# Constant matrix products added ahead of jobs in the mixers of a hybrid decoder step

## What is computed

```python
def mixer(h, lp, st):
    proj = h @ lp['w_in']
    ...
        S_h, o_h = chunk_scan(hgrn_chunk, jnp.zeros((B, H_HGRN, HGRN_DK, HGRN_DV), F32), args_h)
    ...
        (C_m, n_m, m_m), o_m = chunk_scan(mlstm_chunk, init, (q_m, k_m, v_m, ig, lf))
    ...
            o, lse = swa_prompt(q_s[:, :, hs], k_s[:, :, hs], v_s[:, :, hs], win, dil)
    ...
    mix = jnp.concatenate([out_h, out_m, out_s], axis=-1).astype(h.dtype)
    return mix, new_st
```

## Time and profile before

| | us |
|---|---|
| median of 3 runs | 2786.8 (2784.9 to 2788.0) |
| the profiled execution | 2787.2 |
| its span, first to last instruction | 2785.4 |
| mean granted clock | 0.802 |
| first mixers, scores to samples, from the span's start | about 196 to 582 |
| second mixers | about 1257 to 1650 |

### The profile page before, as it was taken

How to read it: one execution, slowest core, us unless ns; L and a number is a source line. 1 busy time by engine, 2 the same in 40 slices (tenths; PEclk the granted TensorE clock), 3 DMA queues, 4 the chain that set the end, 5 groups by cost and what they waited for, 6 DMA issues and landing times.

```text
span 2785.4 us, 38888 instructions
## 1 busy us (share of the span) xinstructions
PE 2360.4 (85%) x15227; PEld 2098.1 (75%) x15227; DVE 1104.0 (40%) x1731; ACT 842.2 (30%) x1211; POOL 620.5 (22%) x323
## 2 busy tenths in 40 slices
PE   6997468776999995998439767899999999999996
PEld 5985266576999994996237556789888898988984
DVE  1113583521110111112576442366474654747542
ACT  3113223223222212112233212435243352533521
POOL 3420340023443442430160011012121121211210
PEclk9995555578999997996555558789898898988986
DMA  3240100011232243221000001145363553635520
GB/s 140 91 137 1 38 1 1 1 64 51 93 98 79 94 148 121 91 90 69 25 14 1 1 34 62 52 153 172 101 204 108 161 162 105 210 104 160 164 90 32
DMA packets 60928, 245.03 MB, mean 88 GB/s; under 512 B 9116, under 2 KB 9852, under 8 KB 60028
## 3 DMA queue, kind: packets, MB, share of 16 engines
q1 hardware_dynamic: 54496, 227.28, 24.8%
q10 hardware_dynamic: 6332, 16.34, 1.6%
HBM read 234.62 MB, written 19.41 MB: 91 GB/s over the span
## 4 chain that ended last, share of the span: by engine, by line
issue 38%; PE 34%; POOL 12%; DVE 10%; ACT 3%; DMA 2%; ACTq 1%; POOLq 0%; DVEq 0%; SPq 0%
PE psum L916 14%; PE psum L956 13%; POOL wlo L486 5%; POOL xlo L361 5%; PE psum L961 2%; PE psum L937 2%; PE psum L1367 2%; DMA wraw<-in_w_in 1%; POOL xnl L492 1%; DVE r_att L1706 1%; PE psum L1420 1%; PE psum L1342 1%; DMA cst<-in_cst 0%; PE psum L1422 0%; DVE r_w L1673 0%
## 5 line engine op out<-in xcount | busy, mean ns | idle before, releaser
L486 POOL TENSOR_TENSOR wlo<-wraw,whi 128x1024 fp32r<-128x1024 f32 (+1 forms) x122 | 304.9, 2501 | 584.4 <-ACT whi L585 584.4
L916 PE MATMUL psum<-xnh,whi 128*128 128x260 f32 x1824 | 373.1, 286 | 56.3 <-POOL wlo L486 21.3
L1420 PE MATMUL psum<-xg,xhi 128*128 128x320 f32 x1408 | 385.8, 316 | 19.7 <-POOL xlo L361 14.3
L361 DVE TENSOR_TENSOR xlo<-xraw,xhi 128x1024 fp32r<-128x1024 f32 (+2 forms) x224 | 282.4, 1264 | 249.4 <-ACT xhi L874 247.5
L1422 PE MATMUL psum<-xg,xlo 128*128 128x256 f32 x1408 | 377.9, 282 | 0.0
L916 PE MATMUL psum<-xnh,wlo 128*128 128x260 f32 x1824 | 370.9, 285 | 0.0
L916 PE MATMUL psum<-xnl,whi 128*128 128x260 f32 x1824 | 370.8, 285 | 0.0
L874 ACT CAST xhi<-xraw 128x1024 fp32r<-128x1024 f32 (+1 forms) x240 | 270.8, 1129 | 270.6 <-PE psum L1422 270.2
L361 POOL TENSOR_TENSOR xlo<-xraw,xhi 128x640 fp32r<-128x640 f32 (+2 forms) x80 | 167.8, 2098 | 815.9 <-ACT xhi L874 815.9
L916 PEld LDWEIGHTS psum<-xnh,whi 128*128 128x128 f32 x1824 | 285.1, 191 | 59.9 <-issue 31.0
L1420 PEld LDWEIGHTS psum<-xg,xhi 128*128 128x128 f32 x1408 | 266.2, 189 | 25.7 <-issue 19.6
(11 more groups left out here) (410 smaller groups left out, 3479.3 us busy)
## 6 DMA issues: line engine op xcount, KB each, us to landing
xraw<-in_moe_gu SPq DMA_DIRECT2D x176, 512.0 KB, 4.2
xraw<-in_moe_dn SPq DMA_DIRECT2D x64, 704.0 KB, 5.4
wraw<-in_w_in SPq DMA_DIRECT2D x54, 512.0 KB, 3.4
wraw<-in_ffn_gu SPq DMA_DIRECT2D x44, 512.0 KB, 3.5
wraw<-in_ffn_dn SPq DMA_DIRECT2D x16, 704.0 KB, 4.1
wraw<-in_w_out SPq DMA_DIRECT2D x16, 512.0 KB, 3.5
out_cache_s<-in_cache SPq DMA_DIRECT2D x4, 2040.0 KB
a_ck<-in_ck ACTq DMA_DIRECT2D x2, 3072.0 KB, 11.7
```

The costliest lines, as they stand in the source:

```text
L361: eng.tensor_tensor(xlo[n % RWX][:, c0:c1], xraw[n % RWX][:, c0:c1], xhi[n % HIX][:, c0:c1].bitcast(F32), ALU.subtract).then_inc(made_, 1)
L486: pool.tensor_tensor(wlo[u % SPL][:, 0:cols], wraw[u % RAW][:, 0:cols], whi[u % SPL][:, 0:cols].bitcast(F32), ALU.subtract).then_inc(lo_ma ...
L916: ins = pe.matmul(out[:, s, :], w[:, k * cols:(k + 1) * cols], x[:, k, s * H2:(s + 1) * H2], start=(k == 0 and first), stop=(k == kt - 1 a ...
L1420: pe.matmul(epart(n), xhi[n % HIX][:, k * P:(k + 1) * P], x_[:, k, :], start=(k == 0), stop=False, skip_group_check=True)
```

## The change

A method `idle(n)` of `Job` multiplies the identity with `mkr` n times into the first 256 columns of the job's own bank. The job's products overwrite these columns afterwards. It is called ahead of the jobs `pv` (12), `kh` (12), the first `at` job of levels 0 to 6 (14), `md` (8) and `mo` (8), in both layers. In the levels the job of the first head is now made ahead of the wait for `lv_made`, with the constant products between its wait for the bank and that one. The wait for `mask_made`, which `mlstm` had, is also made at the start of `window`.

```diff
+                def idle(self, n):
+
+                    for _ in range(n):
+                        pe.matmul(self.out(0, 2 * P), mkr[:, 0, :], mkr[:].rearrange("p a c -> p (a c)"), start=True, stop=True,
+                                  skip_group_check=True)
...
             def window(li):
+                pe.wait_ge(S("mask_made"), 1)
...
                     j = Job(li, "pv", n)
+                    j.idle(12)
                     taken(pe, li, "pt", n, 1 if n < 2 else 0)
...
                     j = Job(li, "kh", c)
+                    j.idle(12)
...
                     if l < LVL:
+                        j = Job(li, "at", 0, l)
+                        j.idle(14)
                         pe.wait_ge(S("lv_made"), LVL * li + l + 1)
...
-                        j = Job(li, "at", h, l)
+                        if h or l == LVL:
+                            j = Job(li, "at", h, l)
...
                     j = Job(li, "md", h)
+                    j.idle(8)
...
                     j = Job(li, "mo", h)
+                    j.idle(8)
                     taken(pe, li, "mqk", h)
```

## The result

The changed kernel takes 2803.5 us (median of 15 runs, 2790.4 to 2817.2) against 2785.7 for the kernel before, measured beside it: ratio 1.0064, 95% interval 1.0049 to 1.0079, or some 18 us slower. The forecast was 55 us slower. The direction and the range held; the size was three times too large.

What follows compares the result with a forecast made beforehand. PE was taken to bound three mixer stages and to be level with DVE in HGRN's levels. Terms 3.5 + 2.5 + 7 + 14.5 = 27.5 us a layer, 55 in both: 2787 + 55 = 2842 us, range 2780 to 2890.

Steps and rivals of the forecast that it cites:

- The price of the products: All bursts: 0.213 us a product at 1.2 GHz, 0.118 at 2.4; 55 us a layer, after cover by waits, without a rise.
- The levels' term: HGRN's seven levels: bursts mostly at 1.2 GHz, part of the products behind them at 2.4; +7 us a layer.
- mLSTM's: mLSTM: two uncovered bursts of 8 a head, 1.2 GHz for nine tenths of the stage; +14.5 us a layer.
- the window's: Window stage, six bursts of 12: half taken between +13.7 (1.2 GHz) and -6.9 (2.4 GHz); +3.5 us a layer.
- the states': HGRN's states and the diagonal: first burst covered, clock rises behind the second; +2.5 us a layer.
- What raises the clock: All bursts: expected to raise the clock where 128-row work stands beside them, 64-row work to lose it; busy PE not enough.
- The fall at 1276: Layer 1's window: clock fell from 1.00 to 0.50 amid gap-free score products, taken as evidence against a lasting high clock.
- the signs that I named: Profile after: mLSTM head about 10.9 us at 0.50, clock changing in kh and window, levels 7 to 8 us apart.
- all at 2.4: Window stage's lower bound: with everything at 2.4 GHz, 6.9 us a layer shorter than before the change.
- No burst raises the clock: Rival for all bursts: they are paid at 1.2 GHz, 55 us a layer, 2897 us; chance 0.11, including a 2873 us variant.
- The clock stays up: Rival for both mixers: bursts keep the clock high, -19 us a layer, outputs up to -13 more; 2745 us, chance 0.14.
- A wash (2787): Rival for all bursts: they lie in PE's waits or the clock pays for them; 2787 us, chance 0.06.

Runs made afterwards that it cites:

- e5_rows5: The changed kernel with all its bursts, but constant products of 5 rows in place of 128; 2904.7 us, ratio 1.0438.
- e1_levels: The changed kernel with only the bursts of 14 ahead of HGRN's levels, the others left out; 2779.8 us, ratio 0.9972.
- e10_levels7: e1_levels with bursts of 7 products in place of 14; 2800.8 us, ratio 1.0060.
- e2_mlstm: The changed kernel with only mLSTM's bursts of 8 (ahead of md and mo), the others left out; 2807.0 us, ratio 1.0072.
- e3_window: The changed kernel with only the bursts of 12 ahead of the pv jobs, the others left out; 2786.3 us, ratio 1.0003.
- e4_states: The changed kernel with only the bursts of 12 ahead of the kh jobs, the others left out; 2784.6 us, ratio 1.0005.
- e7_outputs: e1_levels with a burst of 14 added ahead of each of HGRN's five output jobs; 2785.7 us, ratio 1.0009.
- e9_first24: e1_levels with 24 products ahead of level 0 in place of 14, the other levels unchanged; 2780.4 us, ratio 0.9992.
- e8_best: e1_levels with one burst of 15 added ahead of the first kh job; 2779.7 us, ratio 0.9986.
- e11_levels_again: The same kernel as e1_levels, measured once more in another sitting; 2783.2 us, ratio 0.9995.
- e6_mlstm12: e2_mlstm with bursts of 12 products in place of 8; ratio 1.0030, +9 us.
- e12_mlstm16: e2_mlstm with bursts of 16 products in place of 8; 2794.6 us, ratio 1.0037.

## Why the prediction was right and wrong

The price of the products was right, and so were direction and range. What failed is what the clock gives back, and with it all four terms of the sum: +27.5 us a layer, where the four parts alone measured +8.4. The levels' term is the largest miss (+7 against -2.9 and, measured again, -0.4); mLSTM's was +14.5 against 10.7, the window's +3.5 and the states' +2.5 against 0.3 each.

- **The price of a product: right.** 0.213 us a product at 1.2 GHz gave 55 us a layer for no rise; e5_rows5 took 58.6 in layer 0. A cold head of mLSTM was put at 10.9 us and took 11.0. The first burst of the states is covered, as forecast: the first `su` starts 4.8 us after the keys are there in after (359.06 to 363.86) and 4.7 in before.
- **What raises the clock: right in kind, no rule.** The forecast took rows 5 and 6 to say that operands of 128 rows raise it and a busy PE alone doesn't; e5_rows5 against after bears that out for these bursts. The Trainium skill ("TensorE: Matmul & The Clock Gate", section "Why this matters for your kernels") advises to keep TensorE busy without gaps. By that rule e5_rows5 would have run at full rate; its trace disagrees, with 58.50 of 58.50 us busy at 0.50. The fall at 1276 was misread: in the earlier trace rows it stands between 14 products with vt and the transposes, 1.6 us behind the last scores, and not in their midst. So it doesn't show that 64-row work loses the clock.
- **The levels' term (+7 a layer): wrong in sign.** Two steps failed. "Each burst follows 64-row work and is itself likely still at 1.2" doesn't hold for 14 products a level: the clock stays up through the 64-row products for five levels (after, layer 0, from 402.9 on), and a level with its burst takes 4.9 us, near the 4.5 that the forecast had as its best. And the time behind the last factors was put at nothing: in e1_levels DVE sets the pace up to there, as forecast, but behind them 1.9 us a layer are to be had. Of the signs that I named, levels "about 7 to 8 us apart" throughout appear in e10_levels7 alone.
- **mLSTM (+14.5): right in mechanism, a term mis-sized.** I took 2.4 GHz for a tenth of the stage. In e2_mlstm the mean clock from the first gate products to the samples is 0.61, in after 0.62 and 0.55 over the stage, so between a tenth and a quarter. With e2_mlstm's share of 0.22 the forecast's own bounds (+17.0 to -10.3) give 11.0, an estimate beside the 10.7 measured.
- **Window (+3.5) and states (+2.5): mis-sized.** Alone 0.3 a layer each, which is within what these runs can't tell from nothing. In the window half of the way to "all at 2.4" was taken. In e3_window the mean clock is 0.85 and 0.83, two thirds of the way; from the forecast's bounds (+13.7 to -6.9) that gives -0.3, an estimate. In after it is 0.69 with the same bursts. Why the clock is up more in one execution than in another stays open. In e4_states' profile states and diagonal take 1.4 and 1.2 us more than in before, counted from the first burst: the diagonal gained 1.9 us where 1 was taken.
- **The rivals.** "No burst raises the clock" is e5_rows5, and no other kernel. "The clock stays up" fits most of the levels of e1_levels and layer 1's outputs in e7_outputs, in part of the executions. A wash (2787) is what window and states are by themselves.

The fastest kernels of the study have bursts ahead of the levels and none in mLSTM, window or outputs: medians 0.8 to 5.8 us under before (e1_levels in two sittings, e9_first24, and e8_best with its one burst more). All lie on the same side (ratios 0.9972 to 0.9995), but only e1_levels' first sitting lies past the 0.2% that the prediction took as the least to be told.

## What to carry to other kernels

A constant product put in to lift the clock has one price and two outcomes: compare the engine's time per round, burst included, at either clock with the pace that the next engine sets. In the levels that was 8.8 or 4.9 us against DVE's 6.3, in mLSTM 11.0 against PE's own 7.54, or 6.4 against 8.40, and the dose decided which: try a longer burst before giving up on one, and a shorter one is not the safe choice. Compare a round only with the same round of the kernel before, and look at several executions. Look also for the stretch in which the faster engine can show at all; here it was the two microseconds behind DVE's last factors.

## What the runs showed of the hardware

- A busy PE is not enough: bursts of 128 rows raised the clock, for part of the time, in all stages that the change put them in, bursts of five rows with the same count and columns left it at 0.50 (e5_rows5, mLSTM and levels). Nor are 128 rows enough: the gather, four of whose five products have them, stayed at 0.50 for 25.50 us.
- In these stages the length of a burst decided, not that bursts recur: with 7 a level the levels' products were at 1.2 GHz throughout, with 14 the mean clock of the stage was 0.70 to 0.88 (after, e1_levels, e8_best, e11_levels_again); e2_mlstm with 8 had four of five gate products at 1.2 GHz in each layer, e6_mlstm12 one and two, e12_mlstm16 one and none.
- Forty instructions of 64 rows and 64 columns take 5.62 us at 1.2 GHz and 3.1 at 2.4, so these small products follow the clock nearly in full (a factor of 1.8). The window's score products of 64 rows and 128 columns don't: a pair starts the next product after 0.76 us at either clock (before, layer 1, from 1270.27 and from 1278.25).
- The same instructions come out at different clocks from one execution, or one layer, to the next: the seven levels with 14 products took 38.4, 38.7, 41.8 and 44.5 us, the window stage with its bursts 48.6 and 55.9.
